# A float32 down projection by seven block products in place of eight

## The reference

```python
def conv_glu_ffn(h, w_up, conv_w, conv_b, w_down):
    u = causal_depthwise_conv(h @ w_up, conv_w) + conv_b
    gate, up = jnp.split(u, 2, axis=-1)
    return (jax.nn.gelu(gate, approximate=True) * up) @ w_down
...
        h = rms_norm(x, ffn_pre_norm[l])
        x = x + rms_norm(conv_glu_ffn(h, w_up[l], ...), ffn_post_norm[l])
```

## Time and profile before

| | before |
|---|---|
| median of 3 runs | 1792.47 us (1791.96 to 1797.59) |
| span of the profiled execution | 1791.1 us |
| up projection, dense part | 217 to 354.9 us of the span |
| down projection | 354.9 to 431.2 us |
| TensorE busy, whole span | 1704.2 us (95%) |
| VectorE busy, whole span | 642.6 us (36%) |

### The profile page before, as it was taken

One profiled execution on the slowest core, in us unless ns is written; L12 is line 12 of the kernel. 1 busy time (PEld: TensorE's weight loads), 2 busy tenths in 40 slices (PEclk: granted clock), 3 DMA queues, 4 the chain that ended last, 5 costly groups with the idle time before them and its releaser, 6 DMA issues.

```text
span 1791.1 us, 20952 instructions
## 1 busy us (share of the span) xinstructions
PE 1704.2 (95%) x8474; PEld 977.6 (55%) x8474; DVE 642.6 (36%) x1289; ACT 409.8 (23%) x797; POOL 32.2 (2%) x58
## 2 busy tenths in 40 slices
PE   9999999999999999999899999989899889988897
PEld 8778788887888888888623222322222222222232
DVE  3574466612759999941211101111010101111001
ACT  1143122201263544530111111111110111111112
POOL 4000000000000000100000000000000000000000
PEclk9999999999999999999999999999999999899999
DMA  5340244433453434276799999999999999999998
GB/s 187 118 188 13 83 157 148 163 148 116 166 191 118 168 133 169 104 291 249 304 374 433 433 425 436 430 430 433 431 430 430 430 431 435 430 432 428 432 432 335
DMA packets 36389, 523.07 MB, mean 292 GB/s; under 512 B 3880, under 2 KB 4072, under 8 KB 7784
## 3 DMA queue, kind: packets, MB, share of 16 engines
q1 hardware_dynamic: 35104, 511.75, 69.6%
q10 hardware_dynamic: 1224, 10.50, 1.6%
HBM read 521.12 MB, written 1.12 MB: 292 GB/s over the span
## 4 chain that ended last, share of the span: by engine, by line
PE 71%; DMA 24%; DVE 2%; SPq 1%; ACT 1%; another core or an unknown queue 1%; issue 0%; DVEq 0%; ACTq 0%
DMA arena<-in_experts 24%; PE psum L942 17%; PE psum L1282 13%; PE psum L593 12%; PE psum L1177 5%; PE psum L915 4%; PE psum L1026 3%; PE psum L1231 2%; PE psum L1007 1%; PE psum L1314 1%; PE psum L656 1%; PE psum L677 1%; PE psum L895 1%; PE psum L1201 1%; SPq L476 1%; PE psum L1296 1%
## 5 line engine op out<-in xcount | busy, mean ns | idle before, releaser
L1282 PE MATMUL psum<-arena 128*34 128x512 f32 x1792 | 409.1, 609 | 41.4 <-DMA arena<-in_experts 39.1
L2452 DVE SCALAR_TENSOR_TENSOR arena<-arena,psum 34x512 f32<-34x512 f32 x64 | 44.0, 687 | 758.2 <-ACT arena L1743 758.2
L942 PE MATMUL psum<-arena 128*128 128x272 f32 x1312 | 305.9, 392 | 0.0
L1282 PEld LDWEIGHTS psum<-arena 128*34 128x34 f32 x1792 | 106.2, 113 | 319.7 <-issue 272.9
L942 PEld LDWEIGHTS psum<-arena 128*128 128x128 f32 x1312 | 247.3, 189 | 53.1 <-issue 0.7
L1177 PE MATMUL psum<-arena 128*34 128x512 f32 x896 | 216.4, 639 | 9.8 <-DMA arena<-in_experts 9.8
L593 PE MATMUL psum<-arena 128*128 128x256 f32 x992 | 215.4, 378 | 0.0
L593 PEld LDWEIGHTS psum<-arena 128*128 128x128 f32 x992 | 187.3, 189 | 27.6 <-issue 1.2
L1177 PEld LDWEIGHTS psum<-arena 128*34 128x34 f32 x896 | 57.5, 118 | 157.7 <-issue 157.5
L1743 ACT ACTIVATE arena<-psum 34x512 f32<-34x512 f32 x64 | 37.9, 593 | 441.7 <-PE psum L1282 385.4
L2158 DVE SCALAR_TENSOR_TENSOR arena<-arena 128x272 f32<-128x272 f32 x240 | 111.0, 524 | 3.7
(11 more groups left out here) (444 smaller groups left out, 1367.2 us busy)
## 6 DMA issues: line engine op xcount, KB each, us to landing
arena<-in_experts SPq DMA_DIRECT2D x71, 4096.0 KB, 50.0
arena<-in_panels SPq DMA_DIRECT2D x91, 1024.0 KB, 4.8
arena<-in_experts SPq DMA_DIRECT2D x44, 2048.0 KB, 44.9
arena<-in_down_panels SPq DMA_DIRECT2D x8, 1408.0 KB, 5.9
arena<-in_experts SPq DMA_DIRECT2D x10, 1024.0 KB, 10.7
arena<-scr ACTq DMA_DIRECT2D x4, 2176.0 KB, 8.9
arena<-in_experts SPq DMA_DIRECT2D x4, 512.0 KB, 17.4
out<-arena SPq DMA_DIRECT2D x4, 256.0 KB, 2.1
```

Of the source, the lines that this page charges most:

```text
L942: ins = mm(pair[k][:, b, 0:T], slot8[k][:, c, b * P:(b + 1) * P], src[:, c, :], start=c == 0, stop=c == DC - 1)
L1282: ins = mm(psum[lo:lo + CAP, p % 2, :], xg[:, c, :], r_up[2 * p + x][:, c, :], start=c == 0, stop=c == DC - 1)
L2452: STT(es[gate_at, :], es[gate_at, :], 1.0, psum[gate_at, p % 2, :], ADD, MUL)
```

## The change

The 2816 x 1024 product is split for each of four pairs of output chunks (`i` = 0 to 3) into 2 x 2 blocks: two output chunks, odd and even chunks of the hidden width, and two halves of 128 tokens. Strassen's scheme (in Winograd's form) takes seven block products for each pair in place of eight. Each block product is 11 `mm` calls with 128 tokens. VectorE forms the sums of weight blocks (`down_sums`: S1 to S4, four additions of 128 x 1408 for each `i`) and the sums of activations (t1 to t4, four additions of 128 x 128 in each turn of the gated loop, written over the gate's raw values). Results are combined by VectorE (`keep`, `cross`) and taken by ScalarE from SBUF.

The weights come as 16 quarters of 704 KB in place of eight panels of 1408 KB: the quarters for `i` = 0 and 1 are loaded during the up projection into SBUF that is free then, those for `i` = 2 into the two slots after the last up panel, those for `i` = 3 after the products of `i` = 0 have ended. The gated loop is cut into turns 0 to 3, 4 to 6 and 7 to 10, with `down_sums(0)` and three of the additions of `down_sums(1)` between them. TensorE now waits for 10 turns before its first product and for the eleventh soon after.

```diff
@@ sync @@
+            for j in range(10):
+                panel(PANELS["w_up"] + 2 + j)
+                if j > 1:
+                    quarter((j - 2) // 4, (j - 2) % 4)
+            panels(PANELS["w_up"] + 12, 10)
+            for last in (n[0] - 2, n[0] - 1):
+                sp.wait_ge(panel_done[last % 2], last // 2 + 1)
+            for q in range(4):
+                quarter(2, q)
+            sp.wait_ge(ev("second_done"), 1)
+            for q in range(4):
+                quarter(3, q)
@@ tensor @@
-            for j in range(2):
-                pe.wait_ge(ev("hid_ready"), FB // 4 + 1 if j == 0 else FB // 2)
-                for i in range(4):
...
+            def product(into, weights, tokens, lo, hi, begins, ends):
+                w3 = weights.rearrange("p (m n) -> p m n", m=FB // 2)
+                for m in range(lo, hi):
+                    ins = mm(into, w3[:, m, :], tokens(m), start=begins and m == 0, stop=ends and m == FB // 2 - 1,
+                             skip_group_check=True)
+                return ins
...
+            def first_products(i, lo, hi):
+                pe.wait_ge(ev("sums_ready"), 4 * i + 2)
+                product(sum_of(i, 2), S3[i], combined(2), lo, hi, True, False)
+                product(sum_of(i, 1), S1[i], combined(0), lo, hi, False, False)
+                pe.wait_ge(ev("sums_ready"), 4 * i + 3)
+                return product(sum_of(i, 0), S2[i], combined(1), lo, hi, False, True)
+
+            def second_products(i):
+                pe.wait_ge(ev("kept_ready"), i + 1)
+                pe.wait_ge(ev("sums_ready"), 4 * i + 4)
+                product(sum_of(i, 2), A22[i], combined(3), 0, FB // 2, False, True)
+                product(sum_of(i, 1), S4[i], hidden(1, 1), 0, FB // 2, False, True).then_inc(ev("cross_done"), 1)
+                return product(sum_11[i], A12[i], hidden(1, 0), 0, FB // 2, False, True)
+
+            early = FB // 2 - 1
+            pe.wait_ge(copied[1], n[0] // 2)
+            pe.wait_ge(ev("hid_ready"), early)
+            first_product(0, 0, early)
+            first_products(0, 0, early)
+            first_product(1, 0, early)
+            pe.wait_ge(ev("hid_ready"), FB // 2)
+            first_product(0, early, FB // 2)
+            first_products(0, early, FB // 2).then_inc(ev("first_done"), 1)
+            first_product(1, early, FB // 2)
+            first_products(1, 0, FB // 2).then_inc(ev("first_done"), 1)
+            second_products(0).then_inc(ev("second_done"), 1)
...
+            for i in (2, 3):
+                first_product(i, 0, FB // 2)
+                first_products(i, 0, FB // 2).then_inc(ev("first_done"), 1)
+                second_products(i - 1).then_inc(ev("second_done"), 1)
...
+            pe.wait_ge(ev("second_done"), 3)
...
+            second_products(3).then_inc(ev("second_done"), 1)
@@ vector @@
-                TT(hid[:, bass.ds(i * 2, 2), :], gx, ux, MUL).then_inc(ev("hid_ready"), 1)
-                dve.drain()
-            add_squares("ffn", "sq_added")
+                TT(hid[:, bass.ds(i * 2, 2), :], gx, ux, MUL)
+                dve.drain()
...
+                TT(t3, b22, b12, SUB)
+                TT(t1, b12, b11, SUB)
+                dve.drain()
+                TT(t2, t3, b11, ADD)
+                dve.drain()
+                TT(t4, b21, t2, SUB).then_inc(ev("hid_ready"), 1)
+                dve.drain()
...
+                        ins = TT(S1[i], S3[i], A22[i], ADD)
...
+                        ins = TT(S3[i], A11[i], S3[i], SUB)
...
+                        ins = TT(S2[i], S1[i], A11[i], SUB)
...
+                        ins = TT(S4[i], A12[i], S2[i], SUB)
...
+            with dve.Fori(0, 4) as i:
+                gated_blocks(i)
+            down_sums(0, 0, 4)
+            with dve.Fori(4, 7) as i:
+                gated_blocks(i)
+            down_sums(1, 0, 3)
+            with dve.Fori(7, 11) as i:
+                gated_blocks(i)
+            dve.drain()
+            keep(0)
+            down_sums(1, 3, 4)
+            down_sums(2, 0, 4)
+            keep(1)
+            cross(0)
+            down_sums(3, 0, 4)
+            keep(2)
+            cross(1)
+            keep(3)
+            cross(2)
+            cross(3)
+            add_squares("ffn", "sq_added", 7)
```

More of the change, by code:

```diff
@@ L42 @@
 EB = EFF // P
+QUARTER = FB // 2 * P
 RING = 12
@@ L635, in sum_squares, with sum_added @@
                 ins.then_inc(ev("sum_ready"), 1)
-            def sum_added(bank, count, of):
+            def sum_added(bank, count, of, last=DC - 1):
                 pe.wait_ge(ev("sq_added"), after["sq_added"] + count)
@@ L642, in sum_added @@
                 pe.wait_ge(ev("sq_ready"), SQ[of] + 5)
-                mm(bank[:, 0:S], ones, sq[:, DC - 1, 0:S], start=False, stop=True).then_inc(ev("sum_ready"), 1)
+                mm(bank[:, 0:S], ones, sq[:, last, 0:S], start=False, stop=True).then_inc(ev("sum_ready"), 1)
             def raw_panels(raw, sums, of, width, ready, between=None):
@@ L921, in _, with hidden @@
-            sum_added(pair[0][:, 0, :], 2, "ffn")
+            def product(into, weights, tokens, lo, hi, begins, ends):
[4 more added lines that the diff above has]
+                return ins
+            def hidden(odd, x):
+                return lambda m: hid[:, 2 * m + odd, x * P:(x + 1) * P]
@@ new lines, in combined, with first_product @@
+            def combined(j):
+                return lambda m: raw_gate[:, 2 * (S + 2) * m + j * P:2 * (S + 2) * m + (j + 1) * P]
+            def first_product(i, lo, hi):
+                pe.wait_ge(ev(f"down{i}_loaded"), 64)
+                product(sum_11[i], A11[i], hidden(0, 0), lo, hi, True, False)
+            def first_products(i, lo, hi):
[4 more added lines that the diff above has]
+                return product(sum_of(i, 0), S2[i], combined(1), lo, hi, False, True)
@@ L2064, in _, with gated_blocks @@
             dve.drain()
-            with dve.Fori(0, 11) as i:
+            def gated_blocks(i):
                 for j in range(2):
@@ L2088, in _ @@
                 dve.drain()
-                TT(hid[:, bass.ds(i * 2, 2), :], gx, ux, MUL).then_inc(ev("hid_ready"), 1)
+                TT(hid[:, bass.ds(i * 2, 2), :], gx, ux, MUL)
                 dve.drain()
-            add_squares("ffn", "sq_added")
+                b11, b12, b21, b22 = [hid[:, bass.ds(i * 2 + odd, 1), x * P:(x + 1) * P].rearrange("p a b -> p (a b)")
+                                      for odd in range(2) for x in range(2)]
+                t1, t2, t3, t4 = [raw_gate[:, bass.ds(i * (2 * (S + 2)) + j * P, P)] for j in range(4)]
@@ new lines, in gated_blocks, with down_sums @@
+                TT(t3, b22, b12, SUB)
[5 more added lines that the diff above has]
+                dve.drain()
+            def down_sums(i, first, last):
+                dve.wait_ge(ev(f"down{i}_loaded"), 64)
+                for at in range(first, last):
+                    if at == 0:
+                        ins = TT(S1[i], S3[i], A22[i], ADD)
+                        dve.drain()
+                    elif at == 1:
+                        ins = TT(S3[i], A11[i], S3[i], SUB)
+                        dve.drain()
+                    elif at == 2:
+                        ins = TT(S2[i], S1[i], A11[i], SUB)
+                        dve.drain()
+                    else:
+                        ins = TT(S4[i], A12[i], S2[i], SUB)
+                    ins.then_inc(ev("sums_ready"), 1)
@@ new lines, in keep, with cross @@
+            def keep(i):
+                p11, u2, u3 = [kept[i][:, at * P:(at + 1) * P] for at in range(3)]
+                dve.wait_ge(ev("first_done"), i + 1)
+                CP(p11, sum_11[i])
+                dve.drain()
+                TT(u2, p11, sum_of(i, 0), ADD)
+                dve.drain()
+                TT(u3, u2, sum_of(i, 2), ADD)
+                dve.drain()
+                TT(fT[:, 2 * i + 1, P:S], u3, sum_of(i, 1), ADD).then_inc(ev("kept_ready"), 1)
+            def cross(i):
+                if i < 3:
+                    dve.wait_ge(ev("second_done"), i + 1)
+                else:
+                    dve.wait_ge(ev("cross_done"), 4)
+                u2 = kept[i][:, P:2 * P]
+                TT(fT_flat[:, 2 * i * S + P:2 * i * S + 3 * P].rearrange("p (a b) -> p a b", a=2),
+                   psum[:, 4 + i, P:3 * P].rearrange("p (a b) -> p a b", a=2), bcast(u2, 2, 1), ADD).then_inc(ev("cross_ready"), 1)
```

92 lines of the change are left out of this document (56 added, 36 removed).

## The result

The changed kernel takes 1822.67 us (median of 6 runs, 1818.02 to 1823.28); the kernel before, run beside it, 1795.03 us (6 runs). The ratio is 1.0154, interval 1.0138 to 1.017: slower, as forecast, but 1.7 us above the range. The loss is 27.6 us against these runs and 30.2 against the 1792.47 from which the forecast started; the two medians of the kernel before lie further apart than the 1.7 us by which the range was missed. The profiled spans are 1821.1 and 1791.1 us, so 30.0 us are to be found.

What follows compares the result with a forecast made beforehand. TensorE bounds the kernel; with the change VectorE bounds the up projection. Slower turns and weight sums, less TensorE's saving, plus 1 us of clock end the products 21.0 us later: 1792.5 + 21.0 = 1813.5 us, range 1800 to 1821.

Steps and rivals of the forecast that it cites:

- TensorE's part: Block products: 616 instructions of 128 columns at 111.6 ns, 68.7 us for 76.3, saving 7.6 us if nothing keeps TensorE waiting.
- VectorE's turn: Gated loop: four additions make a turn 12.35 + 1.70 + 0.87 = 14.92 us, more than TensorE's 13.82.
- the weight sums: Between the gated loops: seven additions of 1.62 us with a short pause, 11.7 us, queue everything behind them.
- TensorE's waits: TensorE idle 5 us or more at each of two weight sums, 3 to 4 us before and within the first products.
- the 1 us of clock: Last stretch of products: pauses may lower TensorE's clock; one episode costs 3 us, none nothing, 1 taken.
- The products' end: End of the first block's products: 452.1 us against 431.1 before, 21.0 us later.
- a tail that I had called the same within 0.2: Behind the products: the tail stays the same within 0.2 us, its last square having 128 columns in place of 256.
- The second block follows 1 to 1: Second block: shifts by the first block's full delay, since TensorE is busy for 300 of 300 us in its middle.
- Room in the loop: Rival, gated loop: pauses hide, turns stay 13.82 us, only weight sums count, products 8.6 us late, 1801 us; chance 0.08.
- Weight loads: Rival, block products: weight loads set the pace at 189 ns, products 63.6 us late, 1856 us; chance 0.03.
- Absorbed: Rival, from 880 us: the experts' stream starts at its old time and hides the delay, 1792.5 us; chance 0.05.
- More of the clock: Rival: two low-clock episodes of 3 us and the upper turn of 15.4 us give 1824 us; chance 0.04.

Runs made afterwards that it cites:

- x4: The kernel before with 52 unread TensorE calls between the down projection and the sum of squares; 1815.14 us, ratio 1.0113.
- y1: The changed kernel with 2 unread TensorE calls behind the last product; 1817.5 us, ratio 1.0132 to the kernel before.
- b1: The kernel before with its eleven gated turns written out, nothing else; 1792.05 us, ratio 0.9996.
- x1: The changed kernel without the four additions of activation blocks in each gated turn; 1803.28 us, ratio 1.0048 to the kernel before.
- y2: The changed kernel with 5 unread TensorE calls behind the last product; 1818.86 us, ratio 1.0154 to the kernel before.
- p1: The changed kernel with weight sums for i = 0 and 1 on GpSimd, the gated turns in one loop; 1823.87 us, ratio 1.018 to the kernel before.
- a6: The changed kernel with one panel moved from behind the second block's short products to their middle; 1819.96 us, ratio 1.0137 to the kernel before.
- q3: q2 with one panel moved from behind the second block's short products to their middle; 1790.49 us, ratio 0.9982 to the kernel before.
- q2: The changed kernel with turns written out, seven weight sums in VectorE's waits for ScalarE's logarithm, 80 early calls for 50; 1793.05 us, ratio 0.9993 to the kernel before.

## Why the prediction was wrong

**Right: TensorE's part.** 50.51 / 450 = 112.2 ns a pass against 111.6 taken from the earlier trace rows, with weight loads of 192 ns each (median) beside them; no weight load stood in series. **Right: VectorE's turn.** 14.95 us measured, 14.92 predicted from 12.35 + 1.70 + 0.87; the three parts came out at 12.35, 1.79 and 0.80, so the sum is this close because two small misses cancel. **Right: the weight sums.** 1.63 us each with 0.1 between them; the last turn starts at 380.20, predicted 379.2, 0.3 of it because the first turn started later. **Right in kind, half in size: TensorE's waits.** 7.0 and 6.09 us at the two weight sums, but 2.15 ahead of the first products and 1.86 for the eleventh turn, where the sum has 3.9 and 3.7: the up projection ended at 377.3 us in place of 374.4, and the early calls took 13.03 us in place of 11.2, at a granted clock of 0.52 in their first 3.5 us. The eleventh turn covered both. In the last stretch, for which the 1 us of clock was meant, the granted clock was 1.00 (394.3 to 452.9 us), so that term cost nothing there; the eleventh turn was ready 1.2 us late (394.39 for 393.2). The products' end, 21.7 us late for 21.0, carries a miss of 0.7.

**Wrong: "The second block follows 1 to 1", with 1 us for the clock.** Against the 1792.47 us from which the forecast started, 30.2 us were lost for 21.0 predicted. Of the span's 30.0, 21.7 arose in the first block, 1.1 between the sum of squares and the first mid panel (a tail that I had called the same within 0.2), and 7.2 inside the second block: 3.3 at the short products (26.1 - 22.8) and 4.0 in the routing stage, less 0.1. I had looked for the clock only in the last stretch of the first block and behind pauses, by the earlier trace rows; "TensorE is busy for 300 of 300 us" was taken as proof that a stage only shifts. The stage of short products is busy without a break too, and there the clock fell. x4 and y1 show that neither a later start nor the new scheme forces this.

**What the fall hangs on.** The starts alone give no rule: with the short products in one piece the clock fell there at first panels of 453.9, 455.2, 468.0, 471.4, 475.7 and 481.7 us, and not at 457.4, 458.9, 466.2, 481.3, 481.9, 482.5 and 489.9. The granted clock some 20 us ahead does give one. The changed kernel and y1, right behind TensorE's wait ahead of the second block's first products, and the kernel before across its own:

```profile
457.00:459.00 2.00, 1.57 (x5) 1.04 (x6) 1.83 (x5) 0.66 (x1) 0.00 (x0) 0.79 0.05 12
459.00:461.00 2.00, 2.00 (x5) 1.31 (x5) 1.83 (x5) 0.66 (x1) 0.00 (x0) 0.50 0.00 0
```
```profile
457.00:459.00 2.00, 0.64 (x2) 0.56 (x3) 1.50 (x4) 0.00 (x0) 0.00 (x0) 0.89 0.02 4
459.00:461.00 2.00, 2.00 (x5) 1.44 (x5) 1.73 (x5) 0.75 (x2) 0.00 (x0) 0.50 0.03 8
```
```profile
431.00:460.00 29.00, 25.75 (x109) 19.10 (x108) 18.66 (x40) 8.94 (x17) 1.36 (x10) 1.00 0.21 73
```

All six profiles with a fall at the short products had one here before. Read from windows of 0.5 us, it began 23.1 to 23.7 us ahead of the first mid panel, and the second began 34.1 us behind it in each of the six. y1 and x4 had the first one 23.9 and 24.2 us ahead, and no second; the kernel before, b1, x1, y2 and p1 had neither. a6 and q3 had the first one 23.4 us ahead, within the range of the six, and no second: in these two the split, not the moment, kept the clock up.

What stays open is why the clock falls behind that wait in some kernels. The wait is 2.55 us in q2, which fell, and 2.56 in the kernel before, which did not; it is 2.98 us in the changed kernel, which fell, and in y2, which did not. For the routing stage's 4.0 us no experiment was made; it came and went in the kernels without being touched.

**The rivals.** "Room in the loop" fell with the first turn of 14.95 us. "Weight loads" fell with 112.2 ns. "Absorbed" fell with the experts' 30.1 us. "More of the clock" named the right thing, at the wrong place and with the wrong partner: the two stretches that cost time came in the second block, and the turn stayed at its middle value.

## What to carry to other kernels

A scheme that trades products for additions is priced on the engine that adds, and there the pauses count as well as the additions: writing out the turns took 1.5 of 14.95 us, and seven sums of 1.63 us cost nothing once they lay in a wait of 2.19. A saving or a delay did not pass through the later stages unchanged here, since the granted clock of TensorE fell in them or not by some tenths of a us: look for stretches of short products and for waits behind the change, and test a shift by itself (unread calls are enough) before blaming the change for it. Where the clock had fallen in a stage of short products, cutting it up by a long one took 2.6 us from q2 to q3.

## What the runs showed of the hardware that was not expected

The granted clock fell to its lower level in a stretch where TensorE was busy without a break (3 us of products with weights of 64 or 16 rows, then 0.57, 0.50). It did so in six profiles, each time 34.1 us behind an earlier fall, and not in the seven with the same stretch where the earlier fall was missing or lay at least 0.2 us further ahead of the first mid panel. With the stage split (a6, q3) an earlier fall at the same moment was not followed by a second. GpSimd's float32 addition of 128 x 1408 took 3.16 us, VectorE's 1.63, and four taps of VectorE took 13.05 in place of 1.67 us beside four of them. A loop with computed addresses cost VectorE pauses of 0.2 to 0.3 us ahead of most groups and 0.8 at its turn, 1.5 us in a turn of 14.95 more than the same turns written out.
